# A decoder block's weight ring: one load moved ahead of the x loads, and 16 instead of 8 z/o weight units kept split

## The reference, cut to what matters

```
h = rms_norm(x, norm_g) * (1 + scale) + shift
proj = h @ w_in          # columns: u, z_pool, q, k, v, o, z_mlstm (512 each), gates (8)
pool_out = pool(u) * silu(z_pool)
q, k = silu(conv4(q, k));  hm = mlstm_chunkwise(q, k, v, gates)      # chunks of 128 tokens
mlstm_out = rms_norm(hm) * mh_norm_g * sigmoid(o) * silu(z_mlstm)
x = x + gate * (concat(pool_out, mlstm_out) @ w_out);  out = rms_norm(x, final_g)
```

## Time and profile before

| what | value |
|---|---|
| timed runs | 1773.71, 1779.45, 1781.75 us |
| profiled execution | 1770.55 us, of which 1768.7 us is the span from first to last instruction |
| granted TensorE clock | 0.998 of full speed |
| PE, DVE, ACT, POOL busy | 97%, 72%, 40%, 18% of the span |
| DMA | 385.65 MB, mean 218 GB/s |
| chain that ended last | PE 82%, DVE 7%, DMA 5%, issue 2% |

### The profile page before, as it was taken

One profiled execution on the slowest core, in us unless ns is written; L12 is line 12 of the kernel. 1 busy time (PEld: TensorE's weight loads), 2 busy tenths in 40 slices (PEclk: granted clock), 3 DMA queues, 4 the chain that ended last, 5 costly groups with the idle time before them and its releaser, 6 DMA issues.

```text
span 1768.7 us, 25365 instructions
## 1 busy us (share of the span) xinstructions
PE 1717.9 (97%) x8921; PEld 1468.6 (83%) x8921; DVE 1268.6 (72%) x2591; ACT 713.2 (40%) x1644; POOL 322.8 (18%) x273
## 2 busy tenths in 40 slices
PE   5999989989999999999999999999999999999998
PEld 5888879868898888988889888888889888898886
DVE  7787788656876678765876668766687657776683
ACT  4444253443433435334443434335343353433421
POOL 0023122150220303103130211303021030300300
PEclk9999999999999999999999999999999999999999
DMA  9999965599556984669747796468855598566852
GB/s 336 344 306 339 287 165 191 162 254 284 147 193 190 257 263 112 216 195 280 227 100 242 220 274 175 149 219 227 290 135 200 188 264 255 117 216 199 254 167 83
DMA packets 399698, 385.65 MB, mean 218 GB/s; under 512 B 258300, under 2 KB 292052, under 8 KB 399060
## 3 DMA queue, kind: packets, MB, share of 16 engines
q1 hardware_dynamic: 384340, 361.34, 67.3%
q10 hardware_dynamic: 15232, 22.69, 4.3%
HBM read 321.89 MB, written 62.06 MB: 217 GB/s over the span
## 4 chain that ended last, share of the span: by engine, by line
PE 82%; DVE 7%; DMA 5%; issue 2%; SPq 1%; ACT 1%; POOL 0%; ACTq 0%; POOLq 0%; DVEq 0%
PE ps_acc L723 19%; PE ps_acc L725 18%; PE ps_acc L724 18%; PE ps_num L723 3%; PE ps_num L724 3%; PE ps_num L725 3%; PE ps_kv L723 2%; PE ps_kv L724 2%; PE ps_kv L725 2%; DMA sb_w_split<-w_kept 2%; PE ps_kv L1015 1%; PE ps_num L1009 1%; PE ps_num L1008 1%; PE ps_sco L988 1%; SPq L528 1%
## 5 line engine op out<-in xcount | busy, mean ns | idle before, releaser
L723 PE MATMUL ps_acc<-sb_hT_hi,sb_w_split 128*128 128x512 f32 x1088 | 432.0, 397 | 10.5 <-DMA sb_w_split<-w_kept 7.6
L725 PE MATMUL ps_acc<-sb_hT_hi,sb_w_split 128*128 128x512 f32 x1088 | 424.6, 390 | 0.0
L724 PE MATMUL ps_acc<-sb_hT_lo,sb_w_split 128*128 128x512 f32 x1088 | 423.5, 389 | 0.0
L723 PEld LDWEIGHTS ps_acc<-sb_hT_hi,sb_w_split 128*128 128x128 f32 x1088 | 204.4, 188 | 54.5 <-issue 10.5
L725 PEld LDWEIGHTS ps_acc<-sb_hT_hi,sb_w_split 128*128 128x128 f32 x1088 | 204.2, 188 | 44.1
L724 PEld LDWEIGHTS ps_acc<-sb_hT_lo,sb_w_split 128*128 128x128 f32 x1088 | 204.6, 188 | 39.9
L1522 POOL TENSOR_TENSOR sb_w_split<-sb_w_raw,sb_w_split 128x512 fp32r<-128x512 f32 x92 | 126.1, 1378 | 558.5 <-ACT sb_w_split L1089 558.2
L1089 ACT ACTIVATE sb_w_split<-sb_w_raw 128x512 fp32r<-128x512 f32 x148 | 91.5, 630 | 87.5 <-DMA sb_w_raw<-s_kept 78.2
L2043 DVE SCALAR_TENSOR_TENSOR sb_acc_cv<-sb_shifted,sb_par,sb_acc_cv 128x512 f32<-128x512 f32 x96 | 75.5, 786 | 60.5 <-ACT sb_acc_cv L1346 58.0
L1839 DVE TENSOR_TENSOR sb_w_split<-sb_w_raw,sb_w_split 128x512 fp32r<-128x512 f32 x56 | 55.2, 986 | 76.2 <-ACT sb_w_split L1089 76.1
L1533 POOL TENSOR_TENSOR sb_h_rs<-sb_h_var,sb_mhalf 128x4 f32<-128x4 f32 x32 | 33.9, 1060 | 406.4 <-DVE sb_h_var L2143 406.4
(11 more groups left out here) (289 smaller groups left out, 3817.2 us busy)
## 6 DMA issues: line engine op xcount, KB each, us to landing
sb_w_split<-w_kept SPq DMA_DIRECT2D x280, 512.0 KB, 4.4
sb_w_split<-w_kept SPq DMA_DIRECT2D x56, 520.0 KB, 4.3
sb_w_raw<-s_kept SPq DMA_DIRECT2D x112, 256.0 KB, 4.3
sb_w_raw<-w_in SPq DMA_DIRECT2D x84, 256.0 KB, 4.6
sb_x_res<-x SPq DMA_DIRECT2D x34, 512.0 KB, 4.5
w_kept<-sb_w_split SPq DMA_DIRECT2D x32, 512.0 KB, 4.7
out<-sb_qT SPq DMA_DIRECT2D x32, 512.0 KB, 2.9
sb_x_in<-x SPq DMA_DIRECT2D x112, 128.0 KB, 3.9
```

Source lines behind the costliest of these rows:

```text
L723: pe.matmul(dst, st_hi, mv_hi, start=start, stop=False, skip_group_check=resumed)
L724: pe.matmul(dst, st_hi, mv_lo, start=False, stop=False, skip_group_check=resumed)
L725: return pe.matmul(dst, st_lo, mv_hi, start=False, stop=stop, skip_group_check=resumed)
```

## The change

The first-u-unit load (m = 52) is issued before the wait for product 7 and the x loads, not behind them. `ZO_KEPT` is 16 instead of 8: block 1 also stores units 8 to 15 (products 6 and 5) split, and blocks 2 to 7 load them kept, 512 KB instead of 256 KB each, without their hi and lo work. In block 1 the loads of units 16 to 23 now wait for the stores of units 8 to 15. Which engine makes a lo is unchanged; the counts that are waited for follow.

```diff
-ZO_KEPT = 8
+ZO_KEPT = 16
 ZO_RAW = ZO_UNITS - ZO_KEPT
-ZO_DVE = [u for u in range(ZO_KEPT, ZO_UNITS) if u % 5 in (1, 3)]
+ZO_DVE = [u for u in range(8, ZO_UNITS) if u % 5 in (1, 3)]
...
         def zo_kept_count(u):
-            return len([n for n in KEPT if slot(0, n) == slot(1, QK_END + u)]) + 1
+            return len([n for n in KEPT if slot(0, n) == slot(1, QK_END + u)]) + 1 + u // RING
+
+        def zo_lo_no(units, b, u):
+            late_units = [n for n in units if n >= ZO_KEPT]
+            return units.index(u) + 1 if b == 1 else len(units) + (b - 2) * len(late_units) + late_units.index(u) + 1
...
             def keep_zo(u):
                 m = QK_END + u
-                sp.wait_ge(zo_lo_pool, u + 1)
+                if u in ZO_DVE:
+                    sp.wait_ge(zo_lo_dve, zo_lo_no(ZO_DVE, 1, u))
+                else:
+                    sp.wait_ge(zo_lo_pool, zo_lo_no(ZO_POOL, 1, u))
...
                     if b == 1 and m - 6 - QK_END in range(ZO_KEPT):
                         keep_zo(m - 6 - QK_END)
+                    if QK_END <= m < TILE_UNITS[1]:
+                        load_zo(b, m - QK_END)
+                    else:
+                        load_w(b, m)
                     if m == TILE_UNITS[1] and not last:
                         sp.wait_ge(zo_full, zo_no(b, 7, 1))
                         load_x(b + 1, 0)
                         load_x(b + 1, 1)
-                    if QK_END <= m < TILE_UNITS[1]:
-                        load_zo(b, m - QK_END)
-                    else:
-                        load_w(b, m)
...
                         elif u in ZO_DVE:
-                            pe.wait_ge(zo_lo_dve, (b - 1) * len(ZO_DVE) + ZO_DVE.index(u) + 1)
+                            pe.wait_ge(zo_lo_dve, zo_lo_no(ZO_DVE, b, u))
                         else:
-                            pe.wait_ge(zo_lo_pool, (b - 1) * (len(ZO_POOL) - ZO_KEPT) + ZO_POOL.index(u) + 1)
+                            pe.wait_ge(zo_lo_pool, zo_lo_no(ZO_POOL, b, u))
...
                 def low_zo(u):
-                    if u in ZO_DVE:
+                    if u in ZO_DVE and (u >= ZO_KEPT or b == 1):
```

## The result

The changed kernel took 1800.67 us (median of four runs, 1794.8 to 1802.77), the kernel before beside it on the same chip 1776.58 us: ratio 1.0137, 95% interval 1.0116 to 1.0157. It is slower by 24 us; I had forecast 2 us more, with a range that ended at 1793.

A forecast was written before the change was run, and what follows sets the result against it. PE is busy 97% of the span, so only its idle time can be won, and transfers are near their limit. -6.8 + 3 + 6 = +2.2 us on 1779.45, rounded to 1781.5 us; range 1773 to 1793.

The forecast's parts named there:

- part 2: Blocks 2 to 7: eight more kept loads cost 0.5 us of waits per block, +3 us, bounds 0 to 11.
- Part 1: Start of the u tiles: loading unit 52 before the x loads gains 6.8 us, bounds 5 and 7.6.
- That holds by 0.4 us: Block 2, behind the x loads: unit 53 lands at 615.3, before PE wants it at 615.7.
- the wait only moves: Rival at the u tiles: unit 53 as late as unit 52 was, gain 2 us, 1786 us; chance 0.06.
- The queue ... shrinks by 0.36 us per unit: z/o stage behind unit 15: 3.75 us of extra queue shrinks to about 2 us, unit 20's wait 0.15 us.
- Part 3: Block 1's z/o stage: eight more stores lengthen SP's turns and add store waits, +6 us, from 3 to 11.
- -4 to +9: Whole kernel: the forecast's own range by the bounds, around a sum of +2.2 us.
- bound by transfers: Rival, z/o stage: units 17 and 20 late in blocks 2 to 7, sum +14, 1793 us; chance 0.18.
- p: z/o stage, blocks 2 to 7: transfer pace per unit for units 11 to 15, taken as 1.75 us, between 1.64 and 1.95.

The follow-up runs named there:

- e1: The changed kernel with ZO_KEPT back at 8, so the new load order alone: 1772.98 us, ratio 0.9983 to the kernel before.
- e5: e1 with the two halves of the x loads moved behind units 60 and 61: 1768.44 us, ratio 0.9965 to the kernel before.
- e3: The changed kernel in the old load order, 16 z/o units loaded kept but only 8 stored: 1793.77 us, ratio 1.0092 to the kernel before.
- e14: The changed kernel (16 kept) with its x loads one by one behind units 56 to 63: 1784.92 us, ratio 1.0035 to the kernel before.
- e11: e1 (8 kept) with its x loads one by one behind units 56 to 63: 1766.24 us, ratio 0.9926 to the kernel before.
- e9: Changed kernel, x loads behind units 60 and 61, only hi halves of units 8 to 15 loaded in blocks 2 to 7: 1779.55 us, ratio 1.0006.
- e4: The changed kernel in the old load order, 16 z/o units stored but only 8 loaded kept: 1787.40 us, ratio 1.0053 to the kernel before.
- e10: Changed kernel, x loads behind units 60 and 61, block 1's stores of units 8 to 15 two turns earlier: 1794.87 us, ratio 1.0083.
- e7: The changed kernel with 12 units kept instead of 16: 1781.76 us, ratio 1.0043 to the kernel before.

## Why the prediction was wrong

By the ratios the three parts came out at -3.0, +16.3 and +9.4 us for my -6.8, +3 and +6. All three miss in the same direction, and part 2, the loads, has most of it: 13 of about 21 us.

**Part 1, unit 52 goes ahead of the x loads: the failed step is "That holds by 0.4 us" for unit 53.** Unit 52 behaved as forecast. For unit 53 I took the times of before: x loads from 602.8, 7.37 us long. That is 29.0 us after the stage's first matmul. In the changed kernel they begin when unit 20 has been used, at 30.2 to 32.0, with a queue ahead of them that the kept units have filled, and take 8.6 to 10.0 us. Unit 53 is issued as that ends, and PE waits 1.0 to 2.6 us for it in each of blocks 1 to 6. But e1 shows that the step fails with 8 kept too: gain 3.0 us for my 6.8 (bounds 5 to 7.6), with 5.7 us of waits for units behind the x loads, which there begin at 29.2 to 29.5, as I had it, and take 7.3 to 10.8 us. My rival *the wait only moves* had the mechanism, and I gave it 0.06 because its wait couldn't pass 1 us; that held its landing at the pace of before. The wait reached 3.2 in e1 and 2.6 in after. Moving the burst itself (e5) gives 6 to 7 us, what the step had promised.

**Part 2, the kept loads of blocks 2 to 7: +3 us forecast, bounds 0 to 11; 16.3 by e3, and 9.3 (e14 against e11) without the burst, nearly all inside the stage.** The pace was right: over the five steps from unit 10 to unit 15 it is 1.6 to 1.9 us in blocks 2 to 7, 1.7 in the mean, for my 1.75. Units 11 to 15 land 5.4 to 7.5 us after their issue, where I had 5 to 7 for units 12 to 15. The landing time of unit 15 (issued at 600.76):
```profile
DMA to landing us min/median/max: 6.4/6.4/6.4
```
The step that fails is "The queue ... shrinks by 0.36 us per unit", after which I looked at unit 20 and stopped. How much later a unit lands than before, counted from the stage's first matmul, is 3.6 us at unit 15 in the mean of six blocks (I had 3.75), 2.8 at unit 20 (I had 2, and took off more for the broadcasts), and still 2.8 at unit 24, where 0.36 per unit would have left 0.5. The load of unit 27 is issued 28.6 to 30.0 us after the stage's first matmul, for 27.4 before. Two prices of this I didn't carry on. In the stage the waits are 6.0 us in 14 places in six blocks, twice my 3, up to 1.5 us each: units 16 and 17 cost 0.4 us per block, about the 0.35 that I had for unit 17, units 19 and 20 cost 0.6 for my 0.15. Behind the stage the later and longer x loads make unit 53 late (in the old order unit 52, later than it was), which I had priced with no kept units at all: for part 2 the sum has nothing there, and e3 loses about as much behind unit 20 as before it.

The Trainium skill (DMA: Bandwidth & Descriptors, Specifications) gives about 358 GB/s as a core's limit from HBM, its half of what two cores share. The traces of this kernel, which ran on one core, pass that: 367 GB/s over 8 us of the very mix and 414 GB/s in a stretch of kept loads and one reload of keys. The bytes decide here all the same, as e9 shows.

**Part 3, the stores of block 1: +6 us forecast (3 to 11); 9.4 by e4, 9.4 by the blocks of e14 and e11, 10.0 by those of after and e1.** The term was mis-sized. SP's turns of units 14 to 22 take 2.67 us, in the changed kernel's timeline:
```profile
377.85 0.41 SPq L485 DMA_DIRECT2D sb_w_raw<-s_kept  x1
...
399.17 0.32 SPq L485 DMA_DIRECT2D sb_w_raw<-s_kept  x1
```
(399.17 - 377.85) / 8 = 2.67 for my 2.21 (I had named 2.2 to 2.5 as what to look for). Eight turns are 3.7 us more than I counted as turns, and 2.1 of these are the waits for the stores of units 13 and 14, for which I had added 2 us: the third such wait comes behind unit 22, and the three are 3.4 us. I took the second eight turns to be as long as the first, in a stage whose queue the first had just filled: the stores of units 13 to 15 take 6.1 to 6.9 us to land, for my 4.4 to 4.8. That explains the size of SP's delay; e10, where the waits for stores are gone and the block is as long, shows that SP's turns don't tell the price by themselves.

**Not in the sum at all: the clock.** Three stretches at half clock cost up to 1.6 us each, two of them in block 1; the last section tells what came before them.

**Where the 17.2 us of blocks 2 to 7 are, and what stays open.** The rows of waits show 6.0 + 3.9 us more, and the half clock costs 1.6. The rest is hidden in busy time. The matmul before a wait is drawn with 0.39 us though the next would start after 0.227, and the one behind a waited-for matmul starts 0.34 us after it and not 0.227 (1058.53 for 1058.19). So a wait costs some 0.27 us more than its row says: 4 us with 15 more waits, which makes 15.5 of the 17.2. Counted from start to start of the same matmuls, the traces differ by +10.4 us until the first matmul of unit 20, -6.5 from there to unit 52, +13.0 from unit 52 to unit 54 and 0.2 behind, 17.2 in all. Open is how block 1's price divides between bytes and SP's turns, and why burst and kept units cost more together than each by itself.

**The range.** Added up, the bounds of the three parts give -4.6 and +17 us, and not the "-4 to +9" that stands there. The 24 us measured lie outside either, so the bounds of part 2 were too narrow as well as its value: 11 for the 16.3 of e3.

The rival *bound by transfers* (0.18, 1793 us) was the nearest: right sign, right place, and its own bound of 9 us for block 1. But it had the reason wrong: it decided on p alone, and at the measured 1.7 its price is 0.1 us per block at unit 17. What cost time was the length that the queue kept behind unit 15. So its number was near by luck.

## What to carry to other kernels

When a change puts bytes into a stage whose transfers are already near their limit, follow the queue beyond the next tight unit, to the next burst on the same queue: in e3 half of the price is collected there. Don't take the issue time of a burst from before once the queue ahead of it is longer; here the same eight issues took 7.1 to 10.8 us. And before reordering one load past a burst, ask whether the burst can be spread: with the eight x loads behind eight different units as well (e11) the gain was 12 us, four times what moving the one load gave.

## What the runs showed of the hardware

**Issues on SP took longer where the transfers were backlogged.** The load of a unit took SP 0.49 us at 594.48, in a window with a DMA share of 0.78, and 1.50 at 602.11, in one with 1.09. Eight x loads took 7.1 to 8.7 us in blocks 2 to 6 of before and 8.6 to 10.0 in after. One block of e1, with 8 kept, had 10.8, so the kept units aren't the only reason.

**A wait of two to four microseconds can cost 1.6 us more.** In the traces of before, after and the experiments, between 430 and 1740 us, I took all the PE waits over 1 us, 45 of them. At none of the 26 below 1.9 us did the granted clock fall; of the 19 from 1.94 us on it did at 10, and of the 9 from 2.35 on at 8 (the one of 3.17 us had none). Each time it was 0.5 for 3.4 us and then 1.0 again, and matmuls of 512 columns started every 0.43 us. In block 1's z/o stage, where waits stand close together, it fell behind waits of 1.9 us too (e5 and e7). In e3 it fell at this one:
```profile
1264.49 0.77 PE L734 MATMUL ps_acc<-sb_hT_hi,sb_w_split 128*128 128x512 f32 x1 [3.60 <-DMA sb_w_split<-w_kept]
```
The Trainium skill (TensorE: Matmul & The Clock Gate, Part 1: The HAM clock gate) says that the array's clock is halved after idleness; the trace agrees, with 0.51 and 0.52 granted.

**Loads ran at 414 GB/s**, with a DMA share of 1.02, for 3 us: kept units and one 256 KB reload of keys. The 408 GB/s of the earlier trace rows is of the same mix, not of kept loads alone.
